# The first unit of an output projection, worked on during the last attention head of a two-layer encoder

## The reference

```python
out = lax.map(one_block, qp)                 # softmax attention, 16 heads of 64 values
out = jnp.moveaxis(out, 0, 1).reshape(b, nb * Q_BLOCK, H, V_HEAD_DIM)
return o.reshape(b, L, MLA_HEADS * V_HEAD_DIM) @ w_out     # 1024 x 1024, then h = h + this
...
u = rmsnorm(h, ffn_norm[layer])
h = h + swiglu(u, *[p[layer] for p in ffn_p])
```

## Time and profile before

| what | before |
|---|---|
| median of three runs | 3237.58 us (3236.16 to 3237.85) |
| profiled execution | 3241.2 us |
| its span | 3239.3 us |
| TensorE busy, matmuls | 3139.7 us, 97% |
| VectorE busy | 1790.8 us, 55% |
| ScalarE busy | 789.0 us, 24% |
| GpSimd busy | 1251.1 us, 39% |

### The profile page before, as it was taken

One profiled execution on the slowest core, in us unless ns is written; L12 is line 12 of the kernel. 1 busy time (PEld: TensorE's weight loads), 2 busy tenths in 40 slices (PEclk: granted clock), 3 DMA queues, 4 the chain that ended last, 5 costly groups with the idle time before them and its releaser, 6 DMA issues.

```text
span 3239.3 us, 47102 instructions
## 1 busy us (share of the span) xinstructions
PE 3139.7 (97%) x18782; PEld 2834.2 (87%) x18782; DVE 1790.8 (55%) x2397; ACT 789.0 (24%) x1396; POOL 1251.1 (39%) x566
## 2 busy tenths in 40 slices
PE   8999999899999999999999999799998999999997
PEld 8999999899999999999999987466676888888886
DVE  6677777643333333336788831888877433333335
ACT  4465665611000000002121121333333000000001
POOL 4000000133444444444434443676771444444442
PEclk9999999999999999999999999999999999999998
DMA  3010000121111111112333324232322111111111
GB/s 120 24 42 25 22 25 22 34 88 45 46 45 45 45 45 45 45 46 70 95 96 102 119 98 135 90 117 96 116 84 87 46 45 52 45 45 46 51 46 65
DMA packets 115182, 206.83 MB, mean 64 GB/s; under 512 B 8021, under 2 KB 57429, under 8 KB 115029
## 3 DMA queue, kind: packets, MB, share of 16 engines
q1 hardware_dynamic: 75280, 157.13, 15.2%
q10 hardware_dynamic: 39749, 47.60, 4.5%
HBM read 169.24 MB, written 35.46 MB: 63 GB/s over the span
## 4 chain that ended last, share of the span: by engine, by line
PE 84%; DVE 6%; POOL 4%; issue 4%; ACT 1%; ACTq 0%; DMA 0%; DVEq 0%; POOLq 0%
PE PS L801 77%; PE PS L1055 4%; PE PS L1040 2%; POOL Wlo L719 1%; POOL SQ L764 1%; DVE SS L2055 1%; POOL RMS L729 1%; PE PS L1267 1%; DVE MX L2268 1%; POOL STB L751 0%; POOL SQ L759 0%; PE PS L1415 0%; DVE GD L2638 0%; DVE Ulo L2060 0%; DVE H L2401 0%
## 5 line engine op out<-in xcount | busy, mean ns | idle before, releaser
L674 POOL TENSOR_TENSOR Whi<-Wraw,const 128x1024 fp32r<-128x1024 f32 x185 | 451.5, 2441 | 1779.1 <-PE PS L801 1241.6
L801 PE MATMUL PS<-Uhi,Whi 128*128 128x352 f32 (+1 forms) x2504 | 619.4, 347 | 19.6 <-DVE Ulo L2060 13.9
L801 PE MATMUL PS<-Ulo,Whi 128*128 128x352 f32 (+1 forms) x2504 | 614.4, 345 | 0.0
L801 PE MATMUL PS<-Uhi,Wlo 128*128 128x352 f32 (+1 forms) x2504 | 613.4, 345 | 0.0
L677 POOL TENSOR_TENSOR Wlo<-Wraw,Whi 128x1024 fp32r<-128x1024 f32 x185 | 504.1, 2725 | 14.5
L801 PEld LDWEIGHTS PS<-Uhi,Whi 128*128 128x128 f32 x2504 | 438.2, 189 | 56.8 <-issue 17.2
L801 PEld LDWEIGHTS PS<-Uhi,Wlo 128*128 128x128 f32 x2504 | 441.5, 189 | 31.0
L801 PEld LDWEIGHTS PS<-Ulo,Whi 128*128 128x128 f32 x2504 | 441.7, 189 | 29.9
L2401 DVE TENSOR_TENSOR H<-H,PS 128x1056 f32<-128x1056 f32 (+1 forms) x176 | 217.7, 1237 | 255.1 <-PE PS L801 254.8
L2425 DVE TENSOR_TENSOR HID<-PS,RMS 128x1056 f32<-128x1056 f32 (+1 forms) x44 | 54.6, 1241 | 418.8 <-PE PS L801 418.3
L1791 ACT ACTIVATE HIDhi<-HID 128x1056 fp32r<-128x1056 f32 (+1 forms) x40 | 43.0, 1074 | 888.9 <-DVE HID L2430 888.9
(11 more groups left out here) (288 smaller groups left out, 5158.1 us busy)
## 6 DMA issues: line engine op xcount, KB each, us to landing
Wraw<-in_w SPq DMA_DIRECT2D x211, 512.0 KB, 3.6
xt<-XTT ACTq DMA_DIRECT2D x20, 640.0 KB, 5.9
H<-in_x ACTq DMA_DIRECT2D x16, 528.0 KB, 8.5
Wraw<-in_w SPq DMA_DIRECT2D x32, 256.0 KB, 3.1
zt<-ZB ACTq DMA_DIRECT2D x32, 256.0 KB, 2.0
X<-xt SPq DMA_DIRECT2D x8, 1024.0 KB
Z<-zt SPq DMA_DIRECT2D x32, 256.0 KB, 2.7
KFB<-keyf SPq DMA_DIRECT2D x15, 530.0 KB, 3.7
```

Source lines behind the costliest of these rows:

```text
L674: pool.tensor_tensor(Whi[s][:], Wraw[s][:], ones.unsqueeze(1).broadcast_to([P, BLK, P]), ALU.mult)\
L801: ins = pe.matmul(out, lhsT, rhs, start=start, stop=stop, skip_group_check=True)
```

## The change

Five k tiles of the first unit are worked on behind steps 5 to 9 of the last head, into banks 5 to 7, and the other three in the tail between and behind the last outputs and the last transposition. Both transpositions of the last pair stand behind the last step, one in banks 0 and 1, one in banks 2 and 3. The second unit takes `group(0)`, so that all groups behind it are exchanged; VectorE takes the first unit from banks 5 to 7, and the third unit, which needs bank 5, waits for that (`first_taken`).

```diff
+A_FIRST, FIRST_STEP = 5, 5
+A_LAST_TURN = (0, 2)
...
+        def first_output(kt):
+
+            if kt == 0:
+                now["slot"] = U0_OUT % 2
+                pe.wait_ge(w_full[now["slot"]], c.want(w_full[now["slot"]]))
+                pe.wait_ge(prep_taken, PREP["o", PAIRS - 2, 1] + 1)
+                pe.wait_ge(stats_taken, STATS["q", HEADS - 1] + 1)
+            pe.wait_ge(o_split, c.want(o_split))
+            for p, (W, X) in enumerate(((Whi, Ohi), (Whi, Olo), (Wlo, Ohi))):
+                for n in range(NB):
+                    ins = mm(PS[:, A_FIRST + n, 0:NT], W[now["slot"]][:, kt, :], X[:, kt, n * NT:(n + 1) * NT],
+                             start=(kt == 0 and p == 0), stop=(kt == KD - 1 and p == 2))
+            return ins
...
-                elif n == 8:
-                    turn_outputs(PAIRS - 1, 0)
+                elif n >= FIRST_STEP:
+                    first_output(n - FIRST_STEP)
         t = HEADS * PER_HEAD
         turn_probs(t - 1)
+        turn_outputs(PAIRS - 1, 0, A_LAST_TURN[0])
         outputs(t - 2)
         outputs(t - 1)
-        turn_outputs(PAIRS - 1, 1)
-        now["slot"] = None
-
-
-        for m in range(U_OUT):
+        first_output(KD - 3)
+        turn_outputs(PAIRS - 1, 1, A_LAST_TURN[1])
+        first_output(KD - 2)
+        first_output(KD - 1).then_inc(first_full, 1)
+
+
+        for m in range(1, U_OUT):
+            g = (m + 1) % 2
             enter_unit(U0_OUT + m)
-            pe.wait_ge(grp_free[m % 2], c.want(grp_free[m % 2]))
-            product(group(m % 2), range(KD), Ohi, Olo, range(KD), o_split if m == 0 else None)\
-                .then_inc(to_vector[m % 2], c.adds(to_vector[m % 2]))
+            pe.wait_ge(grp_free[g], c.want(grp_free[g]))
+            if m == 1:
+                pe.wait_ge(prep_taken, PREP["o", PAIRS - 1, 1] + 1)
+            if m == 2:
+                pe.wait_ge(first_taken, 1)
+            product(group(g), range(KD), Ohi, Olo, range(KD))\
+                .then_inc(to_vector[g], c.adds(to_vector[g]))
...
-        b = feed_forward(U0_FFN0, 0, True)
+        b = feed_forward(U0_FFN0, 1, True)
...
-                elif n == 9:
-                    take_outputs_of(PAIRS - 1, 0)
...
         evict(t - 2)
+        take_outputs_of(PAIRS - 1, 0, A_LAST_TURN[0])
         evict(t - 1)
-        take_outputs_of(PAIRS - 1, 1)
+        take_outputs_of(PAIRS - 1, 1, A_LAST_TURN[1])
...
         for m in range(KD):
             vec.wait_ge(x_in[m], c.want(x_in[m], 16))
-            add_to_h(m, m % 2, True)
+            if m:
+                add_to_h(m, (m + 1) % 2, True)
+            else:
+                vec.wait_ge(first_full, 1)
+                step(vec.tensor_tensor(banks(H[:, 0, :]), banks(H[:, 0, :]), PS[:, A_FIRST:A_FIRST + NB, 0:NT], ALU.add))
+                vec.sem_inc(first_taken, 1)
+                vec.sem_inc(h_ready, 1)
             lo_part(m, "ffn0")
...
-        b = feed_forward(0, lambda m: low_u(m, "mix1"), True)
+        b = feed_forward(1, lambda m: low_u(m, "mix1"), True)
```

More of the change, by code:

```diff
@@ L481, in encoder @@
     first_free = sem("first_free")
+    first_full, first_taken = sem("first_full"), sem("first_taken")
     u_half, third_full = [sem(f"u_half{s}") for s in range(NSEQ)], sem("third_full")
@@ L1007, in query_norms, with turn_outputs @@
                 ins.then_inc(stats_full, 1)
-        def turn_outputs(p, s):
+        def first_output(kt):
[10 more added lines that the diff above has]
+            return ins
+        def turn_outputs(p, s, bank=A_PREP):
             pe.wait_ge(o_evicted, 2 * PER_HEAD * p + PER_HEAD + KB * (s + 1))
@@ L1013, in turn_outputs @@
             for b in range(KB):
-                ins = pe.transpose(PS[:, A_PREP + b // 4, b % 4 * CW:(b % 4 + 1) * CW], O[p % 2][:, KB * s + b, :],
+                ins = pe.transpose(PS[:, bank + b // 4, b % 4 * CW:(b % 4 + 1) * CW], O[p % 2][:, KB * s + b, :],
                                    ident[0:CW, 0:CW])
@@ L1697, in evict, with take_outputs_of @@
                            scale=SINV[:, t % RING:t % RING + 1]).then_inc(o_evicted, 1)
-        def take_outputs_of(p, s):
+        def take_outputs_of(p, s, bank=A_PREP):
             act.wait_ge(prep_full, PREP["o", p, s] + 1)
             whole = (KB - 1) * CW
-            act.activation(H[:, p, s * L:s * L + whole], PS[:, A_PREP, 0:whole], ACT.Copy)\
+            act.activation(H[:, p, s * L:s * L + whole], PS[:, bank, 0:whole], ACT.Copy)\
                 .then_inc(act_steps, c.adds(act_steps))
-            act.activation(H[:, p, s * L + whole:(s + 1) * L], PS[:, A_PREP + 1, CW - (L - whole):CW], ACT.Copy)\
+            act.activation(H[:, p, s * L + whole:(s + 1) * L], PS[:, bank + 1, CW - (L - whole):CW], ACT.Copy)\
                 .then_inc(prep_taken, 1)
@@ L1822, in _ @@
             act.dma_start(saved_d[k], H[:, k, :]).then_inc(h_saved, 16)
-        act.wait_ge(to_scalar[0], c.want(to_scalar[0]))
-        act.activation(banks(XC[0:2 * SHEADS, :]), group(0, parts=2 * SHEADS), ACT.Copy)\
+        act.wait_ge(to_scalar[1], c.want(to_scalar[1]))
+        act.activation(banks(XC[0:2 * SHEADS, :]), group(1, parts=2 * SHEADS), ACT.Copy)\
             .then_inc(act_steps, c.adds(act_steps))
         act.wait_ge(act_steps, c.given(act_steps))
-        act.sem_inc(grp_free[0], 1)
+        act.sem_inc(grp_free[1], 1)
         act.sem_inc(dt_raw, 1)
```

## The result

The changed kernel takes 3242.12 us (median of 20 runs, 3240.36 to 3244.88) against 3237.52 for the kernel before (20 runs, 3235.05 to 3241.06): ratio 1.0015, interval 1.0009 to 1.0021. That is 4.6 us more, inside the 0.2% that the prediction called "the same", but 6.0 us above the forecast and 1.0 above the range.

What follows compares the result with a forecast made beforehand. TensorE was taken to bound the kernel; from step 5 to the second unit, terms summed to 29.93 us against 33.26, 3.3 less, or 1.5 less with the clock's fall: 3236.1 us forecast, range 3232.7 to 3241.1.

Steps and rivals of the forecast that it cites:

- What bounds the kernel: Whole span: TensorE is busy almost throughout, so only time off its sequence or a closed hole pays.
- the steps: Last head, steps 5 to 9: moved tiles fill TensorE's idle time; 18.00 us instead of 14.72, 3.97 hidden.
- rival E: Last head: scores still wait for the exponentials, hole unused, step 4.39 us; +2.7 us, 3240.3; chance 0.04.
- The tail: Behind the last step: 3.44 to the last outputs' end, then 1.31, 1.70, 0.62, 3.16 and 1.70 us at full clock.
- the wait for tile 5: Tail, behind the last outputs: TensorE waits 1.31 us for VectorE's low part of tile 5.
- the chain to the last low part: Tail, before tile 7: transposition, two copies, high part, low part take 3.12 us, tile 6 running under it.
- rival D: Behind the projection's first unit: x lands so late that the third unit waits; slower beyond 0.2%; chance 0.03.
- The clock: Tail: TensorE's clock falls to half during narrow work, costing 1.81 us and leaving 1.5 us gain.
- case B: Tail: clock falls and is back by tile 7; −1.5 us, 3236.1, the forecast; chance 0.47.
- case A: Tail: clock stays full, stretch 29.93 us; −3.3 us, 3234.3; chance 0.24.
- Case C: Tail and second unit: clock still at half at tile 7 and as the unit starts; +2.0 us, 3239.6; chance 0.17.
- something else: Any outcome outside the listed cases, to both sides; chance 0.05.

Runs made afterwards that it cites:

- after_again: The changed kernel run once more, unchanged, on another chip: 3241.93 us, ratio 1.0015 to the kernel before.
- after_pad3: The changed kernel with three one-column VectorE copies added in front of the projection's additions: 3235.51 us, ratio 0.9989 to the kernel before.
- after_dt_first: The changed kernel with ScalarE's eviction of the dt product ahead of its eight saves of H: 3235.23 us, ratio 0.9993 to the kernel before.
- before_late: The kernel before with two tiny VectorE operations ahead of tile 5's low part at the first feed-forward's end: 3242.59 us, ratio 1.0017.
- before_dt_first: The kernel before with ScalarE's eviction of the dt product ahead of its eight saves of H: 3236.86 us, ratio 0.9998.
- before_pad1: The kernel before with one one-column VectorE copy added in front of the projection's additions: 3245.24 us, ratio 1.0022.
- before_pad2: The kernel before with two one-column VectorE copies added in front of the projection's additions: 3242.83 us, ratio 1.0011.
- before_exchanged: The kernel before with only the groups of banks exchanged, projection to dt product, and the last transposition in banks 0 and 1: 3236.9 us, ratio 1.0004.

## Why the prediction was wrong

**What bounds the kernel, and the steps:** right. The five steps with tiles took 18.08 us (646.44 − 628.36) against 18.00 forecast, without a pause, so rival E is out.

**The tail:** right, each term within 0.2 us. From the last turning to the end of the last outputs 3.59 against 3.65 (3.44 + 0.21 for the lower clock), the wait for tile 5 1.40 against 1.31, tile 5 2.81 against 2.78, the chain to the last low part 3.11 against 3.12 (655.33 to 658.44), tile 7 1.55 against 1.70. The third unit didn't wait (rival D).

**The clock:** the profiled execution went as case B. It is no property of the kernel: in after_again and after_pad3 the clock stayed at 1.00 and the stretch took 29.98 and 29.99 us, which is case A (29.93), and after_dt_first lay between them with 30.87. Before's own stretch went from 31.76 (before_late) to 33.29 us (before_dt_first). Seven profiles of the old order (33.26, 32.43, 31.97, 31.76, 33.29, and 31.85 and 31.97 in before_pad1 and before_pad2) average 32.4, four of the new (31.68, 29.98, 29.99, 30.87) 30.6, so the gain is about 1.7. That the profiled pair came so near to the forecast (31.68 against 31.8) is partly luck: both executions had the longest time at half clock seen in their order, about 6.8 us. Case C never came. The rule of the Trainium skill on swings between the levels (page "TensorE: Matmul & The Clock Gate", section "A second HAM failure mode: psum-queue depth-cycling"), weighed there, isn't borne out: with pauses of 1.40 and 0.68 the clock was at half for about 6.8 of 8 us (0.58 and 0.57 on average), as long as in the old tail, and with 1.41 and 1.67 in after_again it didn't fall.

**The step that failed:** "Behind it both kernels have the same seven units, and nothing in them changes but which group of banks comes first", with "The flipped groups of banks behind it are symmetrical and cost nothing". The second sentence holds for the banks on the chip (before_exchanged). What the argument left out is that the first unit is no longer counted on its group's semaphore, so that VectorE's program is two instructions longer, one of them ahead of the place of the loss. Together with before_pad1, before_pad2 and after_pad3 this shows that the place of the instructions in the program sets the pause of 0.6 or 0.24 us, that an order of two engines hangs on 0.1 us there, and that ScalarE's eight saves hand the loss on to TensorE. Before already stood 0.10 us from that edge, and the trace showed it: the split behind the addition, and the wait of 0.58 on the dt eviction behind 8.45 us of issues. I read the trace only to 780 us.

That each difference could be put "on the median, since nothing here is proportional", and the 0.05 for something else, were too sure for that reason: the chance of a loss 850 us later was not priced at all. The last sentence of the prediction names a later fall of the clock as a sign of being wrong, but no longer wait, and gives it no price either.

**What stays open:** what the 0.36 us of pause are. The Trainium skill, page "CRC Debugging", section "Comparing the Two Runs", names queue 14 as the sequencers' instruction refill, which would fit a program that crosses into one more refill. But after_pad3 has 50 packets too and no pause there, so the count alone doesn't decide it; no run here shows a refill end where the pause ends. One packet of the queue falls into these rounds, and it lies behind the pause and not in it: it starts 0.69 us behind the start of tile 5's low part in after (1513.81) and 1.06 behind it in before (1518.71), where there is no pause. In after_pad3 it comes one round earlier, behind tile 4's low part (1510.06), so it moves with the place in VectorE's program. Also open is why the clock falls by different amounts behind the same wait (0.97 in after, 0.91 in after_again).

## What to carry to other kernels

Before a change is costed, look in the whole trace for near ties: two engines that start on the same port or buffer within some tenths of a microsecond, with a long queue behind the loser. A change that only shifts instructions can tip one far away, so a loss of this kind is looked for by comparing the lead of one kernel over the other at landmarks along the span. A long list of DMA issues doesn't belong ahead of an eviction for which TensorE waits: here moving it costs nothing that can be measured (3236.86 against 3236.98 us in the kernel before) and takes the edge away, and after it the transposition ahead of tile 5 gives 3233.04 us, below both kernels.

## What the runs showed of the hardware

- The same addition of 128 x 1056 on VectorE takes 1.26 us if it starts 0.1 us ahead of GpSimd's split, and 3.27 if it starts 0.3 to 0.6 behind it. In the first order it is the split that takes longer, 3.42 instead of 2.45.
- With a lead of 0.04 us over the split, VectorE's low part of 128 x 1056 took 3.56 us instead of 1.32, and the split its 2.40 (before_late).
- One copy of a single column, 800 us ahead of the place where it shows, cost 6.5 us; three of them in the changed kernel turned its +4.6 into −3.2.
- Eight DMA issues on ScalarE's queue kept its next activation waiting 8.45 to 9.62 us (before and after_pad3 are the ends).
- Twenty one-column matmuls took 2.39 us at full clock and 4.42 at a fallen one. A wait of about 3.5 us stood ahead of them both times (after, after_again), so its length doesn't decide it.
